# Six slots for raw weights in the first three MLP blocks, one buffer for the shared sums

## What is computed

```python
def mixer_a(h, w_in, w_out):                       # first layer: four products of width 2048
    q, k, v, g = jnp.split(h @ w_in, 4, axis=-1)
    ...
def hybrid_layer(h, ...):                          # last layer
    ...
    h = h + mixed @ w_out
    z = rmsnorm(h, norm2_w) @ mlp_w1               # 2048 -> 8192
    h = h + jnp.square(jax.nn.relu(z)) @ mlp_w2    # 8192 -> 2048
    return h
```

## Time and profile before

| | |
|---|---|
| median of three runs | 2035.51 us |
| the profiled execution | 2033.51 us |
| its span in the profile | 2031.7 us |
| PE busy | 2017.1 us, 99% |
| DVE busy | 1499.1 us, 74% |
| ACT busy | 1281.3 us, 63% |
| DMA engines busy | 59.7% (queue of the loads), 184 GB/s read from HBM |
| granted TensorE clock | 0.999 |

### The profile page before, as it was taken

One profiled execution on the slowest core, in us unless ns is written; L12 is line 12 of the kernel. 1 busy time (PEld: TensorE's weight loads), 2 busy tenths in 40 slices (PEclk: granted clock), 3 DMA queues, 4 the chain that ended last, 5 costly groups with the idle time before them and its releaser, 6 DMA issues.

```text
span 2031.7 us, 25864 instructions
## 1 busy us (share of the span) xinstructions
PE 2017.1 (99%) x9829; PEld 1701.9 (84%) x9829; DVE 1499.1 (74%) x2020; ACT 1281.3 (63%) x1898; POOL 6.1 (0%) x12
## 2 busy tenths in 40 slices
PE   9999999999999999999999999999999999999998
PEld 7888888888898888887889988888888888888886
DVE  6666565788977777788967557877886886797664
ACT  7666666656566688656566445577647746755754
POOL 0000000000000000000000000000000000000000
PEclk9999999999999999999999999999999999999999
DMA  8766555555655555565655556666666565666664
GB/s 263 210 191 196 168 155 158 181 189 177 201 174 184 175 158 149 184 201 168 204 159 156 146 147 194 191 184 199 195 208 196 184 215 182 189 196 204 209 206 146
DMA packets 194784, 375.49 MB, mean 185 GB/s; under 512 B 13875, under 2 KB 48917, under 8 KB 194134
## 3 DMA queue, kind: packets, MB, share of 16 engines
q1 hardware_dynamic: 194662, 373.85, 59.7%
HBM read 371.71 MB, written 2.10 MB: 184 GB/s over the span
## 4 chain that ended last, share of the span: by engine, by line
PE 64%; DVE 3%; ACT 1%; DMA 1%; issue 0%; ACTq 0%; DVEq 0%
PE acc L630 14%; PE acc L632 14%; PE acc L631 14%; PE acc L821 3%; PE acc L823 3%; PE acc L824 3%; PE acc L1143 2%; PE acc L1145 2%; PE acc L1144 2%; PE acc L988 1%; DVE wlo L1956 1%; PE acc L966 1%; PE tp L642 1%; PE tp L988 1%; PE xb L998 1%; DMA raw<-in_mlp_w 1%
## 5 line engine op out<-in xcount | busy, mean ns | idle before, releaser
L1956 DVE TENSOR_TENSOR wlo<-raw,whi 128x1024 fp32r<-128x1024 f32 x612 | 739.9, 1221 | 332.4 <-ACT whi L1330 328.9
L1330 ACT ACTIVATE whi<-raw 128x1024 fp32r<-128x1024 f32 x612 | 644.2, 1058 | 474.9 <-PE acc L632 309.0
L630 PE MATMUL acc<-whi,both 128*128 128x512 f32 (+1 forms) x592 | 226.8, 383 | 0.3 <-DVE wlo L1961 0.3
L632 PE MATMUL acc<-whi,both 128*128 128x512 f32 (+1 forms) x592 | 224.6, 379 | 0.0
L631 PE MATMUL acc<-wlo,both 128*128 128x512 f32 (+1 forms) x592 | 224.4, 379 | 0.0
L630 PE MATMUL acc<-whi,aT 128*128 128x512 f32 x508 | 200.1, 394 | 0.0
L630 PE MATMUL acc<-whi,bT 128*128 128x512 f32 x512 | 199.2, 389 | 0.0
L631 PE MATMUL acc<-wlo,bT 128*128 128x512 f32 x512 | 199.2, 389 | 0.0
L632 PE MATMUL acc<-whi,bT 128*128 128x512 f32 x512 | 199.2, 389 | 0.0
L632 PE MATMUL acc<-whi,aT 128*128 128x512 f32 x508 | 198.1, 390 | 0.0
L631 PE MATMUL acc<-wlo,aT 128*128 128x512 f32 x508 | 197.8, 389 | 0.0
(11 more groups left out here) (518 smaller groups left out, 3815.0 us busy)
## 6 DMA issues: line engine op xcount, KB each, us to landing
raw<-in_mlp_w SPq DMA_DIRECT2D x256, 512.0 KB, 4.2
raw<-in_w_in_a SPq DMA_DIRECT2D x128, 512.0 KB, 3.9
raw<-in_w_ple_gate SPq DMA_DIRECT2D x64, 512.0 KB, 4.0
raw<-in_w_in SPq DMA_DIRECT2D x64, 512.0 KB, 3.8
raw<-in_w_in_b SPq DMA_DIRECT2D x40, 512.0 KB, 4.2
raw<-in_w_out_a SPq DMA_DIRECT2D x32, 512.0 KB, 3.9
raw<-in_w_out_b SPq DMA_DIRECT2D x32, 512.0 KB, 4.4
raw<-in_w_out SPq DMA_DIRECT2D x32, 512.0 KB, 4.4
```

Source lines behind the costliest of these rows:

```text
L630: pe.matmul(o, hi[:, kt, tok], whi[:, slot, wc], start=start, stop=False)
L632: mm = pe.matmul(o, lo[:, kt, tok], whi[:, slot, wc], start=False, stop=stop)
L1330: act.activation(whi[:, u % RING, 0:n], raw[:, u % RING, 0:n], ACT.Copy).then_inc(hi_done, 1)
L1956: dve.tensor_tensor(wlo[:, u % RING, 0:n], raw[:, u % RING, 0:n], whi[:, u % RING, 0:n].bitcast(F32), ALU.subtract).then_inc(lo_done, 1)
```

## The change

Between up0 and down2 a unit goes to one of six raw slots. Slots 4 and 5 lie in memory that other stages use (`more`, of which only the first two and the last two rows of 512 are slots). To make room, `first` has one buffer and not two, so the copy of the first product waits until the sums before it have been added to x, and it is made at unit 13 of its chunk, not at unit 11. `whi` and `wlo` keep four slots. All waits of loads now come from a table, `raw_free`, in which a slot's last user is looked up.

```diff
+DEEP = 6
...
-        first = [sb(f"first{i}", [P, 2, CH], F32, (r3 + 4 * KB, tab_at + 4 * KB)[i]) for i in range(2)]
+        first = sb("first", [P, 2, CH], F32, tab_at + 4 * KB)
+        apart = (r3 - nat_at - 8 * KB) // (2 * KB)
+        more = sb("more", [P, apart + 2, CH], F32, nat_at + 12 * KB)
...
         def quarters(u):
-            return raw[:, u % RING:u % RING + 2, :].rearrange("p s (i n) -> p (s i) n", n=CH)
+            slot = slot_of(u)
+            if slot < RING:
+                return raw[:, slot:slot + 2, :].rearrange("p s (i n) -> p (s i) n", n=CH), (0, 1, 2, 3)
+            return more, (0, 1, apart, apart + 1)
...
+        def slot_of(u):
+            return (u - S["up0"].u0) % DEEP if S["up0"].u0 <= u < S[f"up{PAIRED}"].u0 else u % RING
+
+        held, raw_free, raw_counts = [[] for _ in range(DEEP)], [], []
+        for u in range(units):
+            users = held[slot_of(u)]
+            raw_free.append(users[-1] + 1 if users else 0)
+            users.append(u)
+            raw_counts.append(16 * len(users))
...
                 if u >= RING or not isinstance(r, int):
-                    sp.wait_ge(lo_done, u - RING + 1 + r)
-                dst = raw[:, u % RING, 0:s.kt * s.cols].rearrange("p (k n) -> p k n", k=s.kt)
-                sp.dma_start(dst, unit_source(s, j, uu)).then_inc(raw_full[u % RING], 16)
+                    sp.wait_ge(lo_done, raw_free[u] + r)
+                dst = raw_of(u, 0, s.kt * s.cols).rearrange("p (k n) -> p k n", k=s.kt)
+                sp.dma_start(dst, unit_source(s, j, uu)).then_inc(raw_full[slot_of(u)], 16)
...
+                if b == 0:
+                    sp.wait_ge(sem("pool_split"), 4)
                 stage(f"up{b}")
                 if b == PAIRED:
+                    sp.wait_ge(lo_done, held[DEEP - 1][-1] + 1)
                     sp.wait_ge(sem("zs_lo"), OUT_SUMS + PAIRED * len(SUMMED))
...
                 act.wait_ge(unit_used, u + 1)
-                if n >= len(OUT_PAIRS) + 2:
-                    act.wait_ge(sem("pair_x"), 2 * (n - len(OUT_PAIRS) - 1))
+                if n > len(OUT_PAIRS):
+                    act.wait_ge(sem("pair_x"), 2 * (n - len(OUT_PAIRS)))
...
-                    along(s, j, join({} if j else z_hi(q, 3), {uu + 1: [lambda n=2 * q + j, u=s.u0 + j * s.units + uu: first_product_out(len(OUT_PAIRS) + n, u)]}))
+                    along(s, j, join({} if j else z_hi(q, 3), {uu + 3: [lambda n=2 * q + j, u=s.u0 + j * s.units + uu: first_product_out(len(OUT_PAIRS) + n, u)]}))
```

More of the change, by code:

```diff
@@ L317, in sem @@
             return sems[name]
-        raw_full = [sem(f"raw_full{i}") for i in range(RING)]
+        raw_full = [sem(f"raw_full{i}") for i in range(DEEP)]
         hi_done, lo_done = sem("hi_done"), sem("lo_done")
@@ L383, in shared_of @@
         def shared_of(n):
-            return (out_first, out_second) if n < len(OUT_PAIRS) else (first[n % 2], second)
+            return (out_first, out_second) if n < len(OUT_PAIRS) else (first, second)
         def sums_due(u, after):
@@ L426, in build, with raw_of @@
         V0 = 2 * GKW
-        def raw_count(u):
-            return 16 * (u // RING + 1)
+        def slot_of(u):
[6 more added lines that the diff above has]
+            raw_counts.append(16 * len(users))
+        def raw_count(u):
+            return raw_counts[u]
+        def raw_of(u, lo, hi):
+            slot = slot_of(u)
+            if slot < RING:
+                return raw[:, slot, lo:hi]
+            return more[:, (0, apart)[slot - RING]:, :].rearrange("p i n -> p (i n)")[:, lo:hi]
         def unit_source(s, j, uu):
@@ L1316, in split_to @@
                     kt, cols = shape_of(u)
-                    act.wait_ge(raw_full[u % RING], raw_count(u) + r * 16 // RING if isinstance(r, int) else raw_count(u) + r * (16 // RING))
+                    act.wait_ge(raw_full[slot_of(u)], raw_count(u) + r * 16 // RING if isinstance(r, int) else raw_count(u) + r * (16 // RING))
                     if u >= RING:
@@ L1323, in split_to @@
                     if f and f[1] == 0:
-                        act.activation(whi[:, u % RING, 0:CH], raw[:, u % RING, 0:CH], ACT.Copy).then_inc(hi_done, 1)
+                        act.activation(whi[:, u % RING, 0:CH], raw_of(u, 0, CH), ACT.Copy).then_inc(hi_done, 1)
                     elif cols == 2 * QHEAD:
@@ L1329, in split_to @@
                     elif g is None:
-                        act.activation(whi[:, u % RING, 0:n], raw[:, u % RING, 0:n], ACT.Copy).then_inc(hi_done, 1)
+                        act.activation(whi[:, u % RING, 0:n], raw_of(u, 0, n), ACT.Copy).then_inc(hi_done, 1)
                     else:
@@ L1946, in split_to @@
                         dve.wait_ge(hi_done, u + 1)
-                        dve.tensor_tensor(wlo[:, u % RING, 0:CH], raw[:, u % RING, 0:CH], whi[:, u % RING, 0:CH].bitcast(F32), ALU.subtract).then_inc(lo_done, 1)
+                        dve.tensor_tensor(wlo[:, u % RING, 0:CH], raw_of(u, 0, CH), whi[:, u % RING, 0:CH].bitcast(F32), ALU.subtract).then_inc(lo_done, 1)
                         continue
@@ L1955, in split_to @@
                     elif g is None:
-                        dve.tensor_tensor(wlo[:, u % RING, 0:n], raw[:, u % RING, 0:n], whi[:, u % RING, 0:n].bitcast(F32),
+                        dve.tensor_tensor(wlo[:, u % RING, 0:n], raw_of(u, 0, n), whi[:, u % RING, 0:n].bitcast(F32),
                                           ALU.subtract).then_inc(lo_done, 1)
@@ L1990, in quad_summed @@
             def quad_summed(u, g):
-                sums, four = quads(g)[0], quarters(u)
+                sums, (four, at) = quads(g)[0], quarters(u)
                 if g >= 2:
@@ L1995, in quad_summed @@
                 for v in (u, u + 1):
-                    dve.wait_ge(raw_full[v % RING], raw_count(v))
-                dve.tensor_tensor(sums[:, 0:2, :], four[:, 0:4:3, :], four[:, 1:2, :].to_broadcast((P, 2, CH)), ALU.add).then_inc(sem("quad_step"), 1)
+                    dve.wait_ge(raw_full[slot_of(v)], raw_count(v))
+                dve.tensor_tensor(sums[:, 0:2, :], four[:, 0:at[3] + 1:at[3], :], four[:, 1:2, :].to_broadcast((P, 2, CH)), ALU.add).then_inc(sem("quad_step"), 1)
                 dve.wait_ge(sem("quad_step"), 2 * g + 1)
-                dve.tensor_tensor(sums[:, 2, :], sums[:, 0, :], four[:, 3, :], ALU.add).then_inc(sem("quad_step"), 1)
+                dve.tensor_tensor(sums[:, 2, :], sums[:, 0, :], four[:, at[3], :], ALU.add).then_inc(sem("quad_step"), 1)
                 dve.wait_ge(sem("quad_step"), 2 * g + 2)
-                dve.tensor_tensor(sums[:, 3, :], sums[:, 2, :], four[:, 2, :], ALU.add).then_inc(sem("quad_sums"), 1)
+                dve.tensor_tensor(sums[:, 3, :], sums[:, 2, :], four[:, at[2], :], ALU.add).then_inc(sem("quad_sums"), 1)
             def quad_split(g):
```

## The result

| | before | changed |
|---|---|---|
| median of the runs beside each other (11 each) | 2034.87 us | 2040.43 us |
| lowest to highest | 2032.82 to 2036.68 | 2039.24 to 2041.87 |
| ratio, 95% interval | | 1.0029 [1.0021, 1.0037] |
| profiled execution, its span | 2033.51, 2031.7 | 2041.87, 2040.1 |

The change made the kernel slower by 0.29%, some 5.9 us. 2041.3 was forecast. The clock is granted in full in both profiles (0.999), and PE is busy for 99% of both spans. In the changed kernel's profile L1956, L1330, L630, L821, L493 and L2076 are L1983, L1357, L657, L848, L517 and L2103.

A forecast was written before the change was run, and what follows sets the result against it. PE, busy 99% of the span, bounds the kernel: matmuls at 0.227 us each plus PE's pauses. 6.3 + 0.9 - 1.4 = +5.8 us on the median 2035.51 gives 2041.3 us; range 2036.8 to 2045.5, leaving out 2 in 10.

The forecast's parts named there:

- The gain of the six slots: Down chunks 0: earlier loads remove PE's pauses ahead of unit 12, winning 1.4 us; those ahead of unit 7 stay.
- What costs nothing: MLP: far slots, the `pool_split` wait and the later copy cost nothing; 5.4 us of ACT's idle time cover the copy.
- qk: SP's loop over chunks 1 to 7: four loads wait for the split of unit 8j-1, losing 6.3 us.
- The first chunk: Chunk 1 of qk: unit 8 starts 0.7 to 0.8 us late, and the chunk ends 2.1 us late.
- Boundary 16: qk ahead of unit 16: 4.6 us of slack against 6.5 needed, another 1.9 us lost.
- The loop: qk's boundaries from unit 24 on: a period of 22.2 against 21.8 us, five losses of about 0.45, 2.3 in all.
- The entry: Start of up0: loads of units 450 and 451 wait for later splits, PE pausing 0.8 to 0.9 us ahead of 456.
- The sum: Whole kernel: 6.3 lost in qk plus 0.9 at the MLP's entry less 1.4 gained, +5.8 us.
- The loop's equation: qk: W, the end of unit 8j-1's DVE split, recurs after 15.3 + d; loss once d exceeds 6.4, 6.9 taken.
- rivals 1 and 2: qk's bursts: 1, mild, landing at full rate, 2038.2 us (0.22); 2, slow, d = 8.4, 2049 us (0.10).
- Rival 3: qk's boundaries keep their slack, the wait being satisfied three splits earlier; only the MLP counts, 2035.0 us (0.08).

The follow-up runs named there:

- e3: The changed kernel with qk's loop waits as before and the six slots counted from slot 2, so unit 450 follows unit 446; 2032.23 us, ratio 0.9984.
- e4: The kernel before, with only the loads of units 450 and 451 waiting for two more splits; 2036.10 us, ratio 1.0005.
- e5: The kernel before, with a single buffer for the first product and its copy behind the additions to x; 2034.07 us, ratio 0.9996.
- e8: The kernel before, with late waits only at qk's chunk 1 (units 8 to 11); 2038.17 us, ratio 1.0013.
- e1: The changed kernel, with only qk's loop waiting as before, for each slot's last user; 2032.95 us, ratio 0.9989.
- e6: The kernel before, with loads of units 8j and 8j+1 in qk's loop waiting for the split of unit 8j-2; 2035.25 us, ratio 1.0002.
- e9: The kernel before, with late waits only at qk's chunks 2 to 7 (units 16 to 63); 2037.91 us, ratio 1.0014.
- e2: The kernel before, with each chunk's four first loads in qk's loop waiting for the split of unit 8j-1; 2042.41 us, ratio 1.0030.

## Why the prediction came out right

Step by step, in its own terms:

1. **The gain of the six slots, 1.4: right for the execution I read, too small for the kernel.** The pause ahead of unit 12 went in all three blocks, and that ahead of unit 7 stayed at 0.42. e3's MLP is 1.4 us shorter than before's. The time gives more: e3, which has the six slots and no late wait, is 3.3 us under before [1.4 to 5.1]. Most of the difference shows in the table above. The MLP of the eight profiles with four slots, e4 less its entry's pause of 1.2, takes 688.9 to 690.6 us, and the one I read is the shortest of them. The middle is 689.7, 2.2 above e3, and nearly all of it is pauses for splits, some ahead of other units too. The four profiles with six slots have none but the first pauses. Before's 28 runs lie between 2033.45 and 2038.74 (half of them within 1.3 us), e3's eleven between 2031.60 and 2033.45 (half within 0.4). I read one fast execution as if it were the median. Whether the 1.1 between 2.2 and 3.3 is more of this or noise is not shown.
2. **What costs nothing: right.** e5 measures no change; the copy's new wait is at most 1.6 of the 5.4 us of cover.
3. **qk, 6.3: 6.6 by the stretch.** The wait is the one read (four loads behind one split). The first chunk costs 1.9 (PE's starts of units 8 and 16, and e8's stretch), not 2.1, since unit 8 is 0.6 late and unit 10 0.2. Boundary 16 costs 2.0 of the forecast 1.9. The loop costs 2.7 of 2.3, but not in five equal parts, as the next paragraph shows. By the times e1 and the changed kernel lie 7.5 us apart in their medians. The 0.9 left is about what the later start takes in the changed kernel's profile (1.0 against e1's); whether other executions start as late is not shown.
4. **The entry, 0.9: 1.1 in the changed kernel, 1.2 in e4.** By the times 0.7, e1's median less e3's.
5. **The sum, +5.8: +5.9 [4.3 to 7.5] measured.** The mechanism was right, but that the sum agrees to 0.1 is luck. Both sides were too small and nearly cancel: the gain by 0.8 (profiles) to 1.9 (times), the loss of qk and entry together by 0.5 (profiles: 6.6 + 1.1 against 7.2) to 1.0 (the medians of the changed kernel and e3 lie 8.2 apart). A mended loop shows the gain bare, and only then is it seen.

**The loop's equation** was W' = W + 15.3 + d, with d from the first issue to the third landing. First issues of the seven bursts after are 29.1, 54.0, 76.0, 99.6, 121.7, 143.6 and 165.8; third landings are 6.6, 6.6, 8.3, 6.7, 6.6, 6.8 and 7.4 behind them. 54.0 + 15.3 + 6.6 is 75.9, and 76.0 + 15.3 + 8.3 is 99.6: from 54.0 on the equation holds within 0.1 us at each step. The mean d, 7.0, is near the 6.9 taken, between rivals 1 and 2. Five bursts have the mild one's near-full rate (6.6 to 6.8, landings 1.3 to 1.4 apart), the last has 7.4, and the third has the slow one's 8.3. This one makes the pause of 1.6 at unit 32. No run makes the loads late without joining them, so the queue's part in d is read from the traces and not isolated. The Trainium skill, "DMA: Bandwidth & Descriptors", section "Anatomy of one DMA", fits its 2.0 us plus bytes at 436 GB/s to transfers that GpSimd issues, and SP issues these; carried over to them it gave, as my estimate, 5.6 for a third load and no loss in the loop. None of the seven bursts is below 6.6, and the loss is there.

Rival 3, the other side, falls: e6 shows that it would need the wait just one split earlier, and ACT waits 5.6 us at the boundary.

## What to carry to other kernels

A table of waits worked out for units known at build time must not feed a loop over a register: there "no earlier user" is true of the first pass alone, and here it joined four loads into one burst at every pass. When a ring's depth changes in the middle of a kernel, let the slot numbers run on across the seam, and read the waits on both sides of it. A gain counted from one profile of a kernel with thin slack is the count of that execution: here the seven other profiles of four slots had more such pauses, and with six slots all but the first pauses were gone. Where two profiles are compared, the distance between two fixed instructions gives the loss of a stretch more surely than a sum of its pauses.

## What the runs showed of the hardware

The third burst was slow for a reason I had not thought of. SP's loads at 76.5 and 77.9 of the changed kernel, the second and third of that burst, first by their issue (min/median/max ns), then by their landing, and then the queues from 74 to 80 us:

```profile
L517 SPq DMA_DIRECT2D raw<-in_w_in_a x1: 1170/1170/1170, 76.5 to 76.5; - x1
...
DMA to landing us min/median/max: 6.5/6.5/6.5
```

```profile
L517 SPq DMA_DIRECT2D raw<-in_w_in_a x1: 373/373/373, 77.9 to 77.9; - x1
...
DMA to landing us min/median/max: 6.4/6.4/6.4
```

```profile
q1 hardware_dynamic: 369, 0.72, 41.6%
q8 instruction: 1, 0.02, 1.5%
```

An issue that takes 0.37 to 0.41 us in the other bursts took 1.17, and the load landed 6.5 after it in place of 4.7. A transfer of instructions (16 KB, queue q8) starts at 75.86, 0.1 ahead of the burst. Such transfers come every 24 to 32 us in qk. The burst at 165.8 has one at 165.5, and its second issue took 0.96. In e9 the bursts at 72.7 and 162.2 have one 0.1 to 0.2 ahead and a second issue of 0.94 and 1.12; in e2 those at 76.8 and 166.1, with 1.07 and 0.94. None of the other bursts of these three kernels has one that near, and none has an issue above 0.42. The third loads of these six landed 7.4 to 8.3 us after the first issue, and 6.6 to 6.9 us in the others: the price is 0.7 to 1.7 us per burst.

The rest of the traces says the same. After the first 12 us the twelve profiles hold 62 issues of SP that took more than 0.5 us. All but two of them start between 0.4 us before and 1.9 us after such a transfer, and all 62 come less than 1.5 us behind SP's issue before:

| SP's issues | near a transfer | elsewhere |
|---|---|---|
| less than 1.5 us behind the one before | 60 of 172 above 0.5 us | 2 of 1984 |
| further behind | 0 of 510 | 0 of 6090 |

In these traces loads issued singly are not slowed there, and of those issued together a third are. No run moved the transfer by itself, so what is shown is a coincidence and not a cause, though it holds over all twelve profiles together.
